# Sample attention of a paged decoder step: scores and value products in four column tiles of two heads, placed behind the projection's matmuls

## The reference

```
s = einsum('bqhd,bkhd->bhqk', q, k) * (HEAD_DIM ** -0.5)
s = where(k_pos[None, :] <= q_pos[:, None], s, NEG_INF)
p = softmax(s).reshape(b, N_HEADS, 2, lq, lk)
a = p[:, :, 0] - lam * p[:, :, 1]
o = einsum('bhqk,bkhe->bqhe', a, v)
```

## Time and profile before

| | |
|---|---|
| median of 3 runs | 1945.98 us |
| span of the profiled execution (first to last instruction) | 1942.3 us |
| around the span, median less span | 3.7 us |
| TensorE busy in the span | 1855.0 us (96%) |
| b0 | 75.3 us |
| b1 to b4 together | 388.4 us |
| b5, b6, b7, b8 | 115.5, 105.9, 77.4, 31.5 us |

### The profile page before, as it was taken

How to read it: one execution, slowest core, us unless ns; L and a number is a source line. 1 busy time by engine, 2 the same in 40 slices (tenths; PEclk the granted TensorE clock), 3 DMA queues, 4 the chain that set the end, 5 groups by cost and what they waited for, 6 DMA issues and landing times.

```text
span 1942.3 us, 37404 instructions
## 1 busy us (share of the span) xinstructions
PE 1855.0 (96%) x13315; PEld 1657.8 (85%) x13315; DVE 941.6 (48%) x1412; ACT 712.3 (37%) x1116; POOL 76.8 (4%) x132
## 2 busy tenths in 40 slices
PE   6998999999999889899979999999999999999999
PEld 4998987777777566676649999999999999999998
DVE  4567332323234588684624555444544444445544
ACT  4333222222222435454324444333433344334433
POOL 3000000000000290000000000000000000000000
PEclk9999999999999989899999999999999999999999
DMA  6445466666666545455654455445544555455543
GB/s 171 141 138 180 156 212 225 214 226 204 224 210 227 171 147 170 129 162 184 201 185 155 151 160 163 167 168 163 163 166 168 162 163 166 167 162 164 167 166 135
DMA packets 140971, 337.71 MB, mean 174 GB/s; under 512 B 11339, under 2 KB 11395, under 8 KB 140592
## 3 DMA queue, kind: packets, MB, share of 16 engines
q1 hardware_dynamic: 138688, 332.05, 52.8%
q0 software_dynamic: 2208, 4.74, 0.8%
HBM read 331.64 MB, written 5.96 MB: 174 GB/s over the span
## 4 chain that ended last, share of the span: by engine, by line
PE 88%; DVE 5%; issue 3%; ACT 2%; DMA 1%; DVEq 0%; POOL 0%; ACTq 0%; SPq 0%; POOLq 0%
PE acc L523 21%; PE acc L525 20%; PE acc L524 20%; PE aux L611 12%; PE aux L599 6%; PE aux L651 5%; PE acc L721 1%; DMA page<-in_cache_v 1%; PE acc L743 1%; DVE tmp L1523 1%; DVE w_lo L1211 1%; DVE z L1321 1%; ACT s_rows L982 0%; DVE tmp L1412 0%; PE aux L577 0%
## 5 line engine op out<-in xcount | busy, mean ns | idle before, releaser
L1211 DVE TENSOR_TENSOR w_lo<-raw,w_hi 128x1024 fp32r<-128x1024 f32 x368 | 450.8, 1225 | 533.2 <-ACT w_hi L885 530.4
L885 ACT CAST w_hi<-raw 128x1024 fp32r<-128x1024 f32 x368 | 386.3, 1050 | 649.7 <-PE acc L525 649.7
L523 PE MATMUL acc<-a_hi,w_hi 128*128 128x288 f32 (+1 forms) x1920 | 583.1, 304 | 10.0 <-DVE z L1218 4.0
L525 PE MATMUL acc<-a_hi,w_lo 128*128 128x288 f32 (+1 forms) x1920 | 572.9, 298 | 0.0
L524 PE MATMUL acc<-a_lo,w_hi 128*128 128x288 f32 (+1 forms) x1920 | 572.1, 298 | 0.0
L523 PEld LDWEIGHTS acc<-a_hi,w_hi 128*128 128x128 f32 x1920 | 362.8, 189 | 25.8 <-issue 17.1
L524 PEld LDWEIGHTS acc<-a_lo,w_hi 128*128 128x128 f32 x1920 | 362.8, 189 | 0.5
L525 PEld LDWEIGHTS acc<-a_hi,w_lo 128*128 128x128 f32 x1920 | 363.1, 189 | 0.0
L525 PE MATMUL acc<-h_hi,w_lo 128*128 128x288 f32 x1024 | 302.2, 295 | 0.0
L524 PE MATMUL acc<-h_lo,w_hi 128*128 128x288 f32 x1024 | 301.5, 294 | 0.0
L523 PE MATMUL acc<-h_hi,w_hi 128*128 128x288 f32 x1024 | 301.3, 294 | 0.0
(11 more groups left out here) (202 smaller groups left out, 1004.5 us busy)
## 6 DMA issues: line engine op xcount, KB each, us to landing
page<-in_cache_k SPq DMA_DIRECT2D x128, 512.0 KB, 4.7
page<-in_cache_v SPq DMA_DIRECT2D x128, 512.0 KB, 4.3
raw<-in_w_up SPq DMA_DIRECT2D x128, 512.0 KB, 3.7
raw<-in_w_down SPq DMA_DIRECT2D x128, 512.0 KB, 3.6
raw<-in_w_in SPq DMA_DIRECT2D x80, 512.0 KB, 3.8
raw<-in_w_out SPq DMA_DIRECT2D x32, 512.0 KB, 3.7
out<-y_nat SPq DMA_DIRECT2D x8, 256.0 KB, 2.6
x_nat<-in_x_prompt SPq DMA_DIRECT2D x1, 1024.0 KB, 9.3
```

Of the source, the lines that this page charges most:

```text
L523: mm(out, wh, ah, start=(kt == 0), stop=False)
L525: last = mm(out, wl, ah, start=False, stop=(kt == KT - 1))
L885: nc.scalar.copy(w_hi[:, j % SPL], raw[:, j % RAW]).then_inc(hi_ok, 1)
L1211: v.tensor_tensor(w_lo[:, j % SPL], raw[:, j % RAW], w_hi[:, j % SPL].bitcast(F32), ALU.subtract)\
```

## The change

Scores: head `h` goes to column tile `g = h % 4`, 32 output rows of its own (`GR` = 32). The heads `g` and `g+4` share a tile: `q_cur` now gives each head 32 stationary columns, the head's 8 at offset 0 or 8 and zeros in the others. `aux` 2 and `s_rows` have 128 rows in place of 64, half of them without meaning. Values: four matmuls for each page, one for each column tile, with 16 stationary columns (`GU`) and 256 moving columns (the two heads' values) in place of two with 32 and 512. Turned probabilities are 128 wide, so they go through `aux` 3 in four rounds of 4 pages (steps 0 to 3, evicted by ScalarE, VectorE, ScalarE, VectorE) in place of two rounds of 8. Values run 4 pages behind the keys (`LAG`) in place of 2, and a step's order is turn_keys, middle, products, score, turn_probs, new_keys, values.

```diff
+CG = 4
+HB2 = N_H // CG
+GR = P // CG
+GU = HB2 * QC
+HQ = CG * GR + QC
+LAG = 4
-                for j in range(N_PAGES + 2):
+                for j in range(N_PAGES + LAG):
-                    if vs is not None and j >= 2:
-                        i = j - 2
+                    if vs is not None and j >= LAG:
+                        i = j - LAG
                         load_page(vs, i, False, (pv_mm, KR + N_PAGES * vs + i - KR + 1))
                 for h in range(N_H):
-                    last = mm(aux[0:SC, 2, P * (j % SG):P * (j % SG + 1)], q_cur[:, SC * h:SC * (h + 1)],
-                              kT[:, j % 2, h, :], start=(h == 0), stop=(h == N_H - 1))
+                    g = h % CG
+                    last = mm(aux[GR * g:GR * (g + 1), 2, P * (j % SG):P * (j % SG + 1)], q_flat[:, GR * h:GR * (h + 1)],
+                              kT[:, j % 2, h, :], start=(h < CG), stop=(h >= CG))
-            def turn_probs(s, half):
-                if half == 0:
+            def turn_probs(s, g):
+                if g == 0:
                     pe.wait_ge(o_ok, s + 1)
+                elif g % 2:
+                    pe.wait_ge(pt_a, 2 * s + g // 2 + 1)
                 else:
-                    pe.wait_ge(pt_a, s + 1)
-                for g in (2 * half, 2 * half + 1):
-                    pe.wait_ge(exp_ok, (NG + 1) * s + g + 1)
-                    pe.sem_inc(pe_go, 1)
-                    for j in range(SG * g, SG * (g + 1)):
-                        last = transpose(aux[:, 3, SC * (j % 8):SC * (j % 8 + 1)], s_rows[:, P * j:P * (j + 1)],
-                                         ident[0:SC, 0:SC])
-                    last.then_inc(pt_mm, 1)
+                    pe.wait_ge(pt_d, 2 * s + g // 2)
+                pe.wait_ge(exp_ok, (NG + 1) * s + g + 1)
+                pe.sem_inc(pe_go, 1)
+                for j in range(SG):
+                    last = transpose(aux[:, 3, P * j:P * (j + 1)], s_rows[:, P * (SG * g + j):P * (SG * g + j + 1)], ident[:])
+                last.then_inc(pt_mm, 1)
-                for half in range(2):
-                    rows = slice(SC // 2 * half, SC // 2 * (half + 1))
-                    last = mm(aux[rows, 3, :], pT[:, j, rows], page[:, KR + j % KR, 512 * half:512 * (half + 1)],
-                              start=(j == 0), stop=(j == N_PAGES - 1))
+                v_page = page[:, KR + j % KR, :].rearrange("p (b g e) -> p g b e", b=HB2, g=CG)
+                for g in range(CG):
+                    last = mm(aux[GR * g:GR * g + GU, 3, 0:HB2 * P].rearrange("p (b e) -> p b e", b=HB2), pT[:, j, g, :],
+                              v_page[:, g], start=(j == 0), stop=(j == N_PAGES - 1))
...
                     if ks is not None:
                         turn_keys(ks, j)
-                    if vs is not None and j < 2:
-                        turn_probs(vs, j)
-                    if j >= 1 and ks is not None:
-                        score(ks, j - 1)
-                    if j == 1:
-                        new_keys(vs, ks)
                     if middle:
                         middle(j)
                     if n is not None:
                         products(n, j, a_hi, a_lo, 0, T)
-                    if j >= 2 and vs is not None:
-                        values(vs, j - 2, ks is not None)
+                    if j >= 1 and ks is not None:
+                        score(ks, j - 1)
+                    if vs is not None and j < NG:
+                        turn_probs(vs, j)
+                    if j == LAG:
+                        new_keys(vs, ks)
+                    if j >= LAG and vs is not None:
+                        values(vs, j - LAG, ks is not None)
...
-                    values(vs, N_PAGES - 2, ks is not None)
-                    values(vs, N_PAGES - 1, ks is not None)
+                    for j in range(N_PAGES - LAG, N_PAGES):
+                        values(vs, j, ks is not None)
```

More of the change, by code:

```diff
@@ L161, in build_step @@
             [("kT", [P, 2, N_H, P], F32)])
[L162 to L173, removed]
+        pT = sb("pT", [P, N_PAGES, CG, GU])
+        s_rows = sb("s_rows", [P, PAST + N_SMP])
+        s_max = sb("s_max", [P, NG + 1])
+        s_sum = sb("s_sum", [P, NG + 1])
+        neg_max = sb("neg_max", [P, 1])
+        l_inv = sb("l_inv", [P, 2])
+        pick = sb("pick", [P, 2, HB2, CG, DEC])
+        pick_s = sb("pick_s", [P, HB2, CG, DEC])
+        q_cur = sb("q_cur", [P, HB2, HQ])
+        s_cur = sb("s_cur", [N_SMP, CG, GR // QC, QC])
+        o_rows = sb("o_rows", [P, HB2 * P])
         s_new = sb("s_new", [N_SMP, N_SEQ, N_H, QC])
@@ L685, in body @@
                     pe.wait_ge(or_ok, vs + 1)
-                    for c in range(4):
-                        last = mm(aux[:, 3, 0:N_H * DEC].rearrange("p (a c t) -> p a c t", a=2, c=4)[:, :, c, :],
-                                  o_rows[:, P * c:P * (c + 1)], pick_s[:, :, c, :], start=True, stop=True)
+                    for b in range(HB2):
+                        last = mm(aux[:, 3, CG * DEC * b:CG * DEC * (b + 1)], o_rows[:, P * b:P * (b + 1)],
+                                  pick_s[:, b].rearrange("p c t -> p (c t)"), start=True, stop=True)
                     last.then_inc(ex_mm, 1)
@@ L958, in body @@
                             .then_inc(kT_ok[1], 1)
-                    if vs is not None and j == 0:
-                        act.wait_ge(pt_mm, NG * vs + 2)
-                        nc.scalar.copy(pT[:, 0:8, :], aux[:, 3, :].rearrange("p (j c) -> p j c", c=SC)).then_inc(pt_a, 1)
                     if ks is not None and j % SG == 0 and j:
@@ L968, in body @@
                             hi(n + 1, 0)
+                    if vs is not None and j in (0, 2):
+                        take_probs(j)
                     if beside:
@@ L1367, in body @@
                             lo(n + 1, 0)
+                    if vs is not None and j in (1, 3):
+                        dve.wait_ge(pt_mm, NG * vs + j + 1)
+                        v.tensor_copy(pT[:, SG * j:SG * (j + 1)].rearrange("p j g c -> p (j g) c"), turned_probs)\
+                            .then_inc(pt_d, 1)
                     if beside:
@@ L1379, in body @@
                     dve.wait_ge(pv_mm, KR + N_PAGES * (vs + 1))
[L1380 removed]
+                    v.tensor_copy(o_rows[:], aux[:, 3, 0:HB2 * P]).then_inc(or_ok, 1)
                 if finish:
```

51 lines of the change are left out of this document (29 added, 22 removed).

## The result

| | before | changed |
|---|---|---|
| median | 1945.97 us (1941.73 to 1946.32, 4 runs) | 1782.13 us (1773.93 to 1783.28, 4 runs) |
| ratio | | 0.9155, 95% interval [0.9133, 0.9177] |
| span of the profiled execution | 1942.3 us | 1780.3 us |

The kernel is faster by 8.4%. By spans the gain is 162.0 us where 140 were forecast. The case was right (A: four tiles at once). Several terms of its sum were not, the transfers' above all, and errors of both signs partly cancelled.

The account below looks back on a forecast made before the run. TensorE was taken to bound the kernel, with transfers taking over in b1 to b4. Gains of 21 (b0), 100 (b1 to b4), 14 (b5, b6) and 5 (b7) make 140 us off 1942.3: 1806 as median, range 1782 to 1838.

Parts of the forecast that it names:

- A: Forecast case: four column tiles run at once and transfers bound b1 to b4; 1806 us, chance 0.66.
- The tiles: Scores and values on TensorE: four tiles at once, 0.44 us each, gaining 1.31 and 0.43 us a page.
- B: Rival: weight loads of scores and values are not hidden, 0.6 us more a page; 1827 us, chance 0.11.
- C: Rival: only two column tiles run at a time, a step of 4.65 us; 1850 us, chance 0.11.
- D: Rival: transfers keep only 4.7 us a step in b1 to b4; 1840 us, chance 0.08.
- E: Rival: the four tiles' moving streams take turns, so the kernel gets slower; about 2030 us, chance 0.03.
- The transfers: b1 to b4: 2.5 transfers a step at 1.67 us each allow no step below 4.17 us.
- The end of a body: b1 to b4: about 5 us beyond 16 steps, some 3 of it waiting for value page 15.
- the clock: Sign of failure: granted clock falls where TensorE now waits; b5 and b6 would give back their gain.
- b5, b6: VectorE's waits for the prompt's values shrink, 6 us less in b5 and 8 in b6.
- b7: Only the nine steps ahead of VectorE's layer norm gain, from 3.9 to 3.34 us each: 5 us.
- b8: Last attention stage: bound by transfers, so its gain is 0.

Follow-up runs that it names:

- the kernel with both edits: Changed kernel with value products two a step in steps 10 and 12, their pages issued earlier, and weight chunks two steps later in SyncE's order: 1772.57 us, ratio 0.911.

## Why the prediction was right, and where it failed

**The tiles: right.** "I take four": scores 0.46 us for 0.44 and values 0.55 for 0.44, beside the cost of the changes of shape. In the steady step TensorE takes 3.69 us for 3.78. Scores taken back one after another cost 114 us by the ratios, values in two tiles some 25. B, C, D and E are out: B would need 0.6 us more a page and D a step of 4.7, and nothing of either shows. The Trainium skill's rule that a weight load overlaps matmuls in flight only when its row group differs (TensorE: Matmul & The Clock Gate, Part 3, "What overlaps and what doesn't") doesn't hold here: all these tiles have the same 128 rows, and 16 matmuls with their loads take 0.46 us. The page of the profile before had already spoken against B: matmuls are busy for 96% of the span and weight loads for 85%, so by the records (the matmuls' ends are modelled) the two overlap for most of it, and most of it is projection with 128 rows and 128 columns.

**The transfers: the failed step.** "So a step can't be shorter than 2.5 x 1.67 = 4.17 us" failed. The 1.67 us were read where TensorE waited for every page, and that was taken as proof that the DMA engines could do no more. The DMA share beside it was not at its top. The window of those pages before, share and GB/s last:

```profile
983.00:1004.00 21.00, 13.55 (x55) 2.19 (x56) 0.00 (x0) 0.00 (x0) 0.00 (x0) 1.00 0.92 307
```

And a page there waits for a slot. The chain that ended last in the same window of the kernel before (start, length, what), one round of the four slots:

```profile
988.66 1.08 PE aux L651 x4
...
989.90 4.95 DMA page<-in_cache_v
...
994.89 1.08 PE aux L651 x4
```

Value product 1.08, 0.16 until the page four later is issued, 4.95 until it has landed: 6.23 us for a round of four pages, 1.56 each. In the next round the issue took 1.6 us and the landing 6.08. With 8 slots the last pages come 1.25 us apart, and saturated, with weight chunks between the pages, a transfer takes 1.39 (376 GB/s). The forecast's lower bound of 3.8 a step was the right end. It put 0.48 us too much on each of 64 steps, 31 us in b1 to b4. The next point takes 20 of them back, 5 us for each of four ends, which leaves 11 of the 12.3 measured; the forecast's rounding to 72 us a body is the rest. That the second error takes back two thirds of the first is luck.

**The end of a body: right in kind, mis-sized.** Forecast 5 us over 16 steps of 4.17; measured 69.0 - 16 x 3.69 = 10.0. The wait for page 15 was there (2.0 for 3), and 0.5 to 0.7 us for key page 0 in front of b2 and b3. In b2, which takes 68.4 us, all of TensorE's waits make 3.8 of the 9.4 us beyond 16 steps. Two things were put at nothing in the sum. One is the probabilities' transposes, some 1.9 us in steps 0 to 3. The other is the clock, which the forecast had named as a sign of failure. Step 0 of b2 takes 5.2 us (316.32 to 321.54) without a wait. The windows at the start of b2 and b3:

```profile
316.30:320.00 3.70, 3.67 (x16) 3.68 (x17) 2.75 (x9) 0.59 (x1) 0.00 (x0) 0.50 0.93 328
384.70:388.40 3.70, 3.69 (x16) 3.70 (x17) 2.56 (x9) 0.59 (x1) 0.00 (x0) 0.50 0.96 343
```

The granted clock is 0.50 there, its lower level of 1.2 GHz, behind the waits of 1.99, 0.55 and 0.54 us shown in the end of b1. The keys' transposes take 1.6 us for 0.85 and the projection's slice 3.2 for 1.83, 2.1 us more together, and b4 starts the same way. In the kernel with both edits the longest of these waits is 1.25 us, b2 starts at 1.00, and its step 0 up to the transposes of step 1 takes 3.0 us. The small matmuls of L698 take another 1.0 of the 9.4. Only b1 has waits for the copies of the first `kT`, in step 1 (0.99 and 0.89 us). With the fast steps the queue's order matters as well, and the two causes hide each other.

**b5, b6: right in kind.** VectorE's idle time in front of the prompt's output fell in b6 from 12.8 to 3.8 us, 9.0 for the 8 forecast; its busy time stayed (78.07 and 77.36). That b6 gained 14 comes from more waits than this one: the idle time ahead of the scores' maximum fell from 3.9 to 1.3 too, and VectorE's waits for the new keys' part (2.3) and for the results (2.5) fell to nothing and 0.8. b5 came out at 109.0 for 109.5. The granted clock did fall (0.88 to 0.73 in b5, 0.92 to 0.83 in b6), and they did not give back their gain by it.

**b7: mis-sized.** The layer norm's run is unchanged, and it starts 33.2 us into the body in place of 42.0 (937.83 - 895.80 before):

```profile
772.63 0.69 DVE L1346 TENSOR_REDUCE s_max<-s_rows 128x1 f32<-128x512 f32 x1 [9.57 <-ACT s_rows L959]
773.24 1.94 DVE L1531 RECIPROCAL rstd<-rstd 128x288 f32<-128x288 f32 x1
```

8.8 us for the 5 forecast. The forecast had held these steps to the transfers' 3.34 too. In TensorE's timeline such a step takes 2.0 us where no work of the layer norm stands in it (keys' transposes at 760.09 and 762.11), which is TensorE's own pace of 2.1, and TensorE is busy 13.4 of the 14 us from 759 to 773. It is the same failed term.

**b8: wrong, "0".** It lost 4.5 us. Four rounds through one bank, each waiting for the other engine's copy, replace two, and no projection covers them here. The timeline of the changed kernel:

```profile
806.58 1.09 PE L637 MATMUL aux<-ident,s_rows 128*128 128x128 f32 x4 [0.37 <-DVE o_cache L1409]
808.72 1.08 PE L637 MATMUL aux<-ident,s_rows 128*128 128x128 f32 x4 [1.05 <-ACT pT L964]
810.41 1.08 PE L637 MATMUL aux<-ident,s_rows 128*128 128x128 f32 x4 [0.61 <-DVE pT L1388]
...
815.79 0.29 PE L647 MATMUL aux<-pick_s,s_rows 128*32 128x32 f32 x2 [2.65 <-DVE pT L1388]
818.28 3.62 PE L812 MATMUL aux<-s_new,v_nat 32*128 32x32 f32 x16
```

9.2 us from the first round to the new keys' part, where it was 3.8 (973.25 to 977.00). The granted clock is 0.50 throughout b8, its lower level of 1.2 GHz, after waits of 1.7 and 3.2 us at the end of b7; before, it was 0.89. L812's 16 matmuls take 3.62 us for the 1.97 of the earlier trace rows. The waits for pages behind them take some of this back. How the 4.5 us divide between rounds and clock was not measured apart.

**Small readings.** "Below a third" holds for VectorE in b0 but not in b4, where it is busy 38.62 of 96.10 us; nothing hung on it. And by its own rows 1.9 + 0.5 = 2.4 us of idle time could go from two prompt units of b6, not 2.1: 9.6 in all, with 9.0 measured.

## What to carry to other kernels

A pace read where an engine waits for each transfer can be that of the buffers' round (landing, use and issue, divided by the number of slots). Look for a row with the DMA share near 1.00 before calling it the limit; here the share beside the 1.67 us was 0.92, and 376 GB/s were to be had for its 307. These small fp32 matmuls against a common moving width paid off in four column tiles even though half of the scores' output rows go unused. When a stage gets faster, look at the queue's own order before its bandwidth: two faults that are each enough for a wait show no gain when only one is mended. And read the granted clock beside the waits: in b1 to b4 some 3 us of waits at a body's end were followed by 2 us lost in the steps behind them.

## What was not expected of the hardware

The four tiles' 16 instructions and 16 weight loads came within 0.46 us in both orders of the heads that were tried. A change of tile shape cost 0.20 us (5.77 to 5.57 for one fewer) and 0.12 in another place (scores 0.58 for 0.46 where the values' tiles differ). And where TensorE got faster but had to wait, its granted clock fell: to 0.95 and 0.96 in b1 to b4, where it had been 0.98 to 1.00, and in b5 to b8 from 0.88 to 0.73, 0.92 to 0.83, 1.00 to 0.87 and 0.89 to 0.50. In b5 and b6 VectorE's work set the time, and the stages gained all the same.
